# Second gate's products on ScalarE and its sums on GpSimd, and a new order around the first expert selection, in a two-block kernel on one core

## The chip, the cores and the metric

The kernel runs on 1 core of one Trainium2 chip. The metric is the device time of one execution in microseconds (us). An execution with the profiler on gives the rows that are quoted here; its own time stands beside the median of the runs.

## What is computed

256 tokens of width 1024 pass through a first block of two layers and then through a second block (feed-forward, recurrent and attention parts), which the change doesn't touch. In fp32, one layer of the first block is:

```python
mod = c_act @ w_ada[l] + b_ada[l]                    # 1 x 6144
shift1, scale1, gate1, shift2, scale2, gate2 = split(mod, 6)
h = rms_norm(x, norm1_g[l]) * (1 + scale1) + shift1
x = x + gate1 * (concat(attention, convolution, pooling of h @ w_in[l]) @ w_out[l])
h2 = rms_norm(x, norm2_g[l]) * (1 + scale2) + shift2
x = x + gate2 * peer_ffn(h2)
```

In `peer_ffn` each of 8 heads makes a query per token, scores it against two sets of 128 keys, takes the best 16 of each set and the best 16 of their 256 pairs. Each pair is the number of one of 16384 experts. For each token, head and choice, a row of `peer_u` (4 KB) is gathered and multiplied with h2, and a row of `peer_v` is gathered and added up with the gated result.

## The kernel before, in words

Every engine runs its own program; semaphores join them. Line numbers are those of the kernel before.

**Segments of mod.** A segment (1024 columns of `w_ada`) comes in four pieces, q = 0 to 3, of 1 MB each (L495), into the upper halves of the four ring slots. For each half k of a piece, DVE adds piece times a column of `c_act` to a sum held per partition (L2290 in `later_part`, 1024 elements a partition); the first addition starts from `bias_pad`. When all eight are done, `segment_ready` is given, and PE *spreads* the segment: a product with ones adds up the partitions and gives the sum to all of them (`spread`, L1583, 4 rows of the trace). The result is in PSUM, where ScalarE copies it (L952) or DVE takes it with the gain (`scaled_gain`, L2309). A piece's place is given back by `ada_free[q]`, and SP fills it with the next piece in its own fixed order: second gate (GATE2), gain, weights of head 0, next layer's SCALE1, weights of heads 1 to 3, next layer's SHIFT1, weights of heads 4 to 7. SP waits at each for its place.

**From the output rows to the first selection.** PE multiplies the output weights (L1533): first what ends the rows of tile 0 (tokens 0 to 127) and then those of tile 1, with two spreads (L1588) between. DVE, in order: the sums of GATE2 (first piece, `scaled_gain` of SCALE2, three pieces), then per tile: x plus gate times rows (`add_gated`, L2171 and L2173), one sum for the next layer's SCALE1 (`next_first(1)`, L2478), and, when ScalarE has the root mean square (L876, L878), the normalising in two steps (L2114, L2119). ScalarE stands at its copy of SHIFT2 (L952) before it takes tile 0's mean square. PE turns a tile (L1429), makes its queries for head 0 (L1766) and scores them (L1772); between tiles 0 and 1 it spreads GATE2. DVE finds the best keys of tile 0 (L2500 to L2508, per set) and the best pairs (L2513 to L2543), and gives the expert numbers; GpSimd then issues the gathers (L753 for `peer_u`, L759 for `peer_v`), 128 rows or 0.5 MB each.

**After it.** DVE makes six more sums of SCALE1, waits for PE's spread of it (`scaled_gain` from bank 6), makes the eight of SHIFT1, and starts with the dot products (L2577). PE, behind tile 1, waits to spread SCALE1 and then goes through heads 1 to 7 (L1795, `query`; L1808, `key_products`). Part of the gathers has places only when PE is through with a head's weights (`weights_used`). Layer 1 has no next layer in the first block: SCALE1 and SHIFT1 and their spreads fall away there.

**GpSimd** has a convolution and a pooling (L710 to L744) and is then idle up to the first gather.

Of the kernel before, what the change touches and what calls it, by code (L numbers as in the profile page):

```python
# [17 lines left out]
ALU = mybir.AluOpType  # L18
# [9 lines left out]
D = 1024  # L28
KC = D // P
# [46 lines left out]
def program(nc, A, out):  # L76
    with ExitStack() as ctx:
# [3 lines left out]
        def sem(name):  # L81
            return ctx.enter_context(nc.semaphore(name))
# [322 lines left out]
        gelu_ready, rnn_out_ready = sem("gelu_ready"), sem("rnn_out_ready")  # L405
        wf_ready = sem("wf_ready")
        zeroed_for_act = sem("zeroed_for_act")
        f_by_head, f_turned = qk_done, qk_turned
# [60 lines left out]
        def _(sp):  # L469
# [14 lines left out]

            def bias_row(l, segment, pad):
                sp.dma_start(pad[0:1, :], A["b_ada"][l:l + 1, segment * D:(segment + 1) * D]).then_inc(bias_in, 16)

# [27 lines left out]
            for l in range(DEPTH):  # L515
# [37 lines left out]
                for u in range(4):  # L553
                    later_piece(l, SHIFT2, u)
                segment_bias(l, GATE2)
                for q in range(ADA_PAIRS):
                    later_piece(l, GATE2, q)
                w_q = of("peer_wq").rearrange("(k p) n -> p k n", p=P)
# [94 lines left out]
        def _(pool):  # L653
# [53 lines left out]
            for l in range(DEPTH):  # L707
# [35 lines left out]
                pool.sem_inc(pool_steps, -steps.reset())  # L743
                g.tensor_tensor(pooled[:], pooled[:], zc[:, 6:8, :], ALU.subtract).then_inc(pooled_ready, 1)  # L744


# [117 lines left out]
        def _(act):  # L864
# [89 lines left out]
            for l in range(DEPTH):  # L954
# [111 lines left out]
                a.activation(table_use[:], eps[:], ACT.Sqrt).then_inc(act_steps, 1)  # L1066
                act.wait_ge(act_steps, steps.next())
                spread(mod[:, SHIFT2, :], 2)
                norm_x_tile(0)
# [344 lines left out]
        def _(pe):  # L1414
# [167 lines left out]

            def spread(source, bank, give, alone=True):  # L1583

                pe.wait_ge(segment_ready, 1)
                pe.sem_inc(segment_ready, -1)
                for c in range(2):
                    ins = mm(ps[:, bank + c, :], ones[:], source[:, c * N:(c + 1) * N], start=alone, stop=True)  # L1588
                ins.then_inc(give, 1)
# [12 lines left out]
            for l in range(DEPTH):  # L1602
# [176 lines left out]
                first_head(0, w_first)  # L1779
                spread(mod[:, GATE2, :], 2, spread_for_act)  # L1780
                turn_h_tile(1, WORK)
                first_head(1, w_first)
                if l + 1 < DEPTH:
                    spread(mod[:, 0, :], 6, spread_for_dve)
                job = 4
# [26 lines left out]

                query(1)
                for head in range(2, EXPERT_HEADS):
                    query(head)
                    key_products(head - 1)
                    if l + 1 < DEPTH and head == 3:
                        pe.wait_ge(spread_taken, 1)
                        pe.sem_inc(spread_taken, -1)
                        spread(gain_post, 6, spread_for_act)  # L1820
# [270 lines left out]
        def _(dve):  # L2091
# [287 lines left out]
            for l in range(DEPTH):  # L2379
# [73 lines left out]
                more = l + 1 < DEPTH  # L2453
                later_part(0, mod[:, GATE2, :])
                dve.wait_ge(post_in, 16)
# [3 lines left out]
                if l + 1 == DEPTH:  # L2459
                    dve.sem_inc(post_free, 1)  # L2460
                for q in range(1, ADA_PAIRS):
                    later_part(q, mod[:, GATE2, :])
                take_mod()
# [24 lines left out]
                for t in range(TILES):  # L2488
# [6 lines left out]
                    if t == 0:  # L2495
                        take_mod()
                    normalise_tile(t, mod[:, SCALE2, :], mod[:, SHIFT2, :])
                def best_keys(s, scored=half_s):

# [61 lines left out]
                if more:  # L2561
                    next_first(6)
                    dve.wait_ge(pre_in, 16)
# [3 lines left out]
                    dve.sem_inc(u_free, 1)  # L2567
                    next_first(8)
                    assert not first_parts
# [426 lines left out]
```

## Time and profile before

| | |
|---|---|
| median of 3 runs | 2767.92 us (2764.54 to 2772.52) |
| profiled execution | 2766.92 us, span 2765.2 |
| busy over the span | PE 87%, DVE 74%, GpSimd 38%, ScalarE 28% |
| HBM over the span | 293 GB/s |
| layer 0, layer 1 of the first block | about 0 to 840 us, 840 to 1640 us |

The page has a line of slices, each digit the busy share of a fortieth of the span in tenths; it shows in which stretches the DMA engines are full. The view by stretches gives the same for any stretch, with the bytes moved. The timeline gives the instructions of one engine in order of time; in brackets stands how long the engine was idle before, and what ended that. An engine's name with q is its own queue: the wait was for a semaphore at that line.

### The profile page before, as it was taken

The page shows a single profiled execution, that of the slowest core. Times are in us where ns is not written, and L with a number is a line of the kernel's source. Part 1 is how long each engine was busy: PE and PEld are TensorE (multiplying, and loading weights), DVE is VectorE, ACT ScalarE, POOL GpSimd, SP SyncE. Part 2 cuts the span into 40 slices and gives each one's busy share as a digit, 9 for nine tenths or more (in the row PEclk, how much of TensorE's full clock was granted, in tenths as well). Part 3 has the DMA queues.
Part 4 walks back from the last instruction along what each step waited for, and adds up shares of the span by engine and source line. Part 5 has one row for each costly group of instructions (what it writes and reads, how often), then busy time and mean ns, then how long its engine had stood idle before and what let it go on. Part 6 is the DMA issues. An engine that isn't in the chain of part 4 may idle for free. (4 is left out here: it accounts for less than half of the span.)

```text
span 2765.2 us, 31596 instructions
## 1 busy us (share of the span) xinstructions
PE 2401.3 (87%) x9946; PEld 1612.3 (58%) x9946; DVE 2048.1 (74%) x3778; ACT 770.8 (28%) x1088; POOL 1056.0 (38%) x1144
## 2 busy tenths in 40 slices
PE   6979877787778989777778778999999999998998
PEld 5666333333335775333333336888878898887787
DVE  7877788787787876778778777667777656655765
ACT  3422011011012322101100114446543444345443
POOL 1336777777772336777777770002000000000000
PEclk9989998888889999999989889999999999999999
DMA  9789999999999789999999997664466655652564
GB/s 354 253 315 367 409 410 410 409 409 410 410 401 345 253 301 365 409 410 410 409 409 410 410 401 222 195 181 120 141 177 191 191 161 175 190 175 69 158 184 137
DMA packets 424192, 812.71 MB, mean 294 GB/s; under 512 B 26024, under 2 KB 262130, under 8 KB 424094
## 3 DMA queue, kind: packets, MB, share of 16 engines
q0 software_dynamic: 147968, 537.84, 49.2%
q1 hardware_dynamic: 276126, 273.62, 31.3%
q8 instruction: 54, 0.88, 0.1%
q14 instruction: 44, 0.36, 0.0%
HBM read 810.32 MB, written 1.05 MB: 293 GB/s over the span
## 5 line engine op out<-in xcount | busy, mean ns | idle before, releaser
L1833 PE MATMUL ps<-weight_ring,arena 128*128 128x512 f32 x1616 | 810.3, 661 | 254.6 <-PEq L1830 152.2
L1833 PEld LDWEIGHTS ps<-weight_ring,arena 128*128 128x128 f32 x1616 | 339.1, 214 | 720.6 <-issue 720.6
L2577 DVE CUSTOM_DVE_ANT_0 arena<-arena,ps 128x1024 f32<-128x1024 f32 x384 | 455.8, 1218 | 164.5 <-DMA arena<-in_peer_u,expert 145.4
L1466 PE MATMUL ps<-hT_pair,w_hi 128*128 128x512 f32 x1312 | 461.5, 396 | 7.4 <-PEq L1860 7.2
L2137 DVE TENSOR_TENSOR ring_lo<-weight_ring,w_hi 128x3072 fp32r<-128x3072 f32 (+1 forms) x102 | 325.4, 3191 | 172.0 <-DVEq L2136 171.9
L759 POOL DMA_INDIRECT weight_ring<-in_peer_v,expert x390 | 373.0, 956 | 121.2 <-issue 69.6
L753 POOL DMA_INDIRECT arena<-in_peer_u,expert x360 | 341.8, 949 | 134.9 <-issue 54.0
L1465 PE MATMUL ps<-hT_pair,ring_lo 128*128 128x256 f32 x1148 | 320.7, 279 | 0.0
L1466 PEld LDWEIGHTS ps<-hT_pair,w_hi 128*128 128x128 f32 x1312 | 240.8, 188 | 57.1 <-issue 10.1
L921 ACT ACTIVATE w_hi<-weight_ring 128x3072 fp32r<-128x3072 f32 (+1 forms) x102 | 267.7, 2626 | 8.8 <-ACTq L920 8.7
L1130 ACT ACTIVATE acts<-dots 128x8 f32<-128x8 f32 x64 | 13.2, 209 | 865.9 <-ACTq L1129 865.8
L1465 PEld LDWEIGHTS ps<-hT_pair,ring_lo 128*128 128x128 f32 x1148 | 216.6, 189 | 7.1
L2606 DVE TENSOR_SCALAR arena<-ident,acts,gate 128x128 f32<-128x128 f32 x500 | 136.7, 371 | 63.9 <-DVEq L2601 63.9
L860 POOL MEMSET arena<- 128x4096 f32 x1 | 3.5, 3518 | 448.1 <-POOLq L859 448.1
L1457 PE MATMUL ps<-hT_pair,ring_lo 128*128 128x256 f32 (+1 forms) x496 | 139.7, 282 | 0.0
L1203 ACT ACTIVATE arena<-arena 128x256 f32<-128x256 f32 x84 | 35.1, 418 | 307.7 <-ACTq L1202 307.4
L2577 DVE CUSTOM_DVE_ANT_0 weight_ring<-weight_ring,ps 128x1024 f32<-128x1024 f32 x96 | 113.7, 1217 | 5.7 <-DMA weight_ring<-in_peer_u,expert 5.7
L1833 PE MATMUL ps<-hT,arena 128*128 128x512 f32 x256 | 115.2, 593 | 0.5 <-PEq L1830 0.5
L1533 PE MATMUL ps<-w_hi,ff_hi 128*128 128x512 f32 x352 | 109.9, 392 | 0.0
L1533 PE MATMUL ps<-ring_lo,ff_hi 128*128 128x512 f32 x352 | 109.2, 390 | 0.0
L1533 PE MATMUL ps<-w_hi,ff_lo 128*128 128x512 f32 x352 | 109.1, 389 | 0.0
L2727 DVE TENSOR_REDUCE arena<-ps 128x512 f32<-128x1024 f32 x84 | 102.4, 1220 | 4.5 <-DVEq L2726 4.2
(404 smaller groups left out, 3943.6 us busy)
## 6 DMA issues: line engine op xcount, KB each, us to landing
weight_ring<-in_w_ada SPq DMA_DIRECT2D x48, 1024.0 KB, 7.5
weight_ring<-in_ffn_w_gate SPq DMA_DIRECT2D x88, 512.0 KB, 4.0
weight_ring<-in_ffn_w_up SPq DMA_DIRECT2D x88, 512.0 KB, 5.3
weight_ring<-in_ffn_w_down SPq DMA_DIRECT2D x88, 512.0 KB, 5.8
weight_ring<-in_peer_wq SPq DMA_DIRECT2D x16, 1024.0 KB, 9.6
weight_ring<-in_w_in SPq DMA_DIRECT2D x14, 1024.0 KB, 7.7
weight_ring<-in_rg_w_in SPq DMA_DIRECT2D x12, 896.0 KB, 5.2
weight_ring<-in_w_out SPq DMA_DIRECT2D x8, 1024.0 KB, 7.5
```

The source lines that it names most:

```text
L753: g.indirect_dma_start(u_place(l, k), None, A["peer_u"], bass.IndirectOffsetOnAxis(chosen_by[p][:, k:k + 1], 0)).then_inc(u_in[k], 16)
L759: g.indirect_dma_start(v_place(l, k), None, A["peer_v"], bass.IndirectOffsetOnAxis(chosen_by[p][:, k:k + 1], 0)).then_inc(v_in[k], 16)
L921: a.activation(hi[slot][:, 0:width], ring[:, slot, 0:width], ACT.Copy).then_inc(w_hi_ready, 1)
L1457: ins = mm(where, w_low, s_high, start=False, stop=(k == len(pairs) - 1))
L1465: mm(where, w_low, s_high, start=False, stop=False)
L1466: ins = mm(both, w_high, s_pair, start=(k == 0), stop=last)
L1533: ins = mm(ps[:, banks + 2 * t + c, :], source[:, t * P:(t + 1) * P], w[:, c * N:(c + 1) * N], start=start and i == 0, stop=stop and i == ...
L1833: ins = mm(ps[:, 2 * t + c, :], diag[:, k, :], v_place(l, k)[:, c * N:(c + 1) * N], start=False, stop=False, skip_group_check=True)
L2137: v.tensor_tensor(ring_lo[:, slot, 0:width], ring[:, slot, 0:width], hi[slot][:, 0:width].bitcast(F32), ALU.subtract).then_inc(w_split, 1)
L2577: ins = v.tensor_tensor_reduce(out=row, in0=row, in1=h_rows(t), scale=1.0, scalar=0.0, op0=ALU.mult, op1=ALU.add, accum_out=dots[:, g, j:j ...
L2606: v.tensor_scalar(diag[:, k, :], ident[:], acts[:, g, j:j + 1], gate[:, k:k + 1], ALU.mult, ALU.mult).then_inc(diag_ready, 1)
L2727: v.tensor_reduce(gu_sum, banks, AX_X, ALU.add).then_inc(gu_summed, 1)
```

## The change

GATE2's eight products move to ScalarE (each piece times its column, written over the piece), behind its table load and ahead of its copy of SHIFT2. GATE2's eight sums move to GpSimd, behind the pooling, and it gives the pieces' places and the bias row back. The semaphores for it are ones of the second block. PE's spread of GATE2 waits for GpSimd's. DVE, now without GATE2, goes on to `add_gated` of tile 0; three more sums of next layer's SCALE1 follow tile 0's normalising, the rest of them the first selection, and `scaled_gain` comes after half of SHIFT1's sums. PE spreads SCALE1 behind head 1 instead of ahead of it.

```diff
@@ names
+        gate2_in = [gates_ready, root_in, root_ready, gelu_ready]
+        gate2_bias_in, gate2_scaled, gate2_ready = rnn_out_ready, exp_ready, abs_ready
@@ SP
-                segment_bias(l, GATE2)
+                sp.wait_ge(bias_free, 1)
+                sp.sem_inc(bias_free, -1)
+                bias_row(l, GATE2, bias_pad, gate2_bias_in)
                 for q in range(ADA_PAIRS):
-                    later_piece(l, GATE2, q)
+                    sp.wait_ge(ada_free[q], 1)
+                    sp.sem_inc(ada_free[q], -1)
...
+                    sp.dma_start(ada_piece(SLOTS + q), src[:, 2 * q:2 * q + 2, GATE2 * D:(GATE2 + 1) * D]).then_inc(gate2_in[q], 16)
@@ GpSimd, behind the pooling
+                gate2 = mod[:, GATE2, :]
+                pool.wait_ge(gate2_bias_in, 16)
+                pool.sem_inc(gate2_bias_in, -16)
+                for q in range(ADA_PAIRS):
+                    for k in range(2):
+                        pool.wait_ge(gate2_scaled, 1)
+                        pool.sem_inc(gate2_scaled, -1)
+                        g.tensor_tensor(gate2, ada_piece(SLOTS + q)[:, k, :], bias_pad[:] if q == 0 and k == 0 else gate2,
+                                        ALU.add).then_inc(pool_steps, 1)
+                        pool.wait_ge(pool_steps, steps.next())
+                    pool.sem_inc(ada_free[q], 1)
+                    if q == 0:
+                        pool.sem_inc(bias_free, 1)
+                pool.sem_inc(gate2_ready, 1)
+                pool.sem_inc(pool_steps, -steps.reset())
@@ ScalarE
                 act.wait_ge(act_steps, steps.next())
+                for q in range(ADA_PAIRS):
+                    act.wait_ge(gate2_in[q], 16)
+                    act.sem_inc(gate2_in[q], -16)
+                    for k in range(2):
+                        piece = ada_piece(SLOTS + q)[:, k, :]
+                        a.activation(piece, piece, ACT.Copy, scale=c_act[:, 2 * q + k:2 * q + k + 1]).then_inc(gate2_scaled, 1)
                 spread(mod[:, SHIFT2, :], 2)
                 norm_x_tile(0)
@@ PE
-                spread(mod[:, GATE2, :], 2, spread_for_act)
+                spread(mod[:, GATE2, :], 2, spread_for_act, ready=gate2_ready)
                 turn_h_tile(1, WORK)
                 first_head(1, w_first)
-                if l + 1 < DEPTH:
-                    spread(mod[:, 0, :], 6, spread_for_dve)
...
                 query(1)
+                if l + 1 < DEPTH:
+                    spread(mod[:, 0, :], 6, spread_for_dve)
                 for head in range(2, EXPERT_HEADS):
@@ DVE
-                later_part(0, mod[:, GATE2, :])
                 dve.wait_ge(post_in, 16)
...
-                for q in range(1, ADA_PAIRS):
-                    later_part(q, mod[:, GATE2, :])
                 take_mod()
...
                     normalise_tile(t, mod[:, SCALE2, :], mod[:, SHIFT2, :])
+                    if t == 0:
+                        next_first(3)
...
                 if more:
-                    next_first(6)
+                    next_first(3)
+                    next_first(4)
                     dve.wait_ge(pre_in, 16)
                     dve.sem_inc(pre_in, -16)
                     scaled_gain(gain_pre[:], 6, gain_pre[:])
                     dve.sem_inc(spread_taken, 1)
                     dve.sem_inc(u_free, 1)
-                    next_first(8)
+                    next_first(4)
```

## Rows read from the trace of the kernel before

**Rows 1.** Stretches; columns: stretch, length, busy of each engine (count), PEclk, DMA share, GB/s.

```profile
158.00:170.00 12.00, 7.78 (x50) 6.08 (x50) 9.99 (x28) 3.79 (x9) 1.25 (x1) 0.99 0.00 0
...
230.00:240.00 10.00, 9.98 (x58) 8.94 (x57) 10.00 (x25) 2.59 (x6) 5.46 (x6) 1.00 0.71 231
240.00:250.00 10.00, 9.22 (x25) 4.26 (x24) 3.04 (x8) 1.83 (x3) 7.56 (x9) 1.00 0.95 339
250.00:800.00 550.00, 429.82 (x884) 182.03 (x883) 432.81 (x1111) 50.47 (x96) 412.22 (x432) 0.88 1.03 410
```

**Rows 2.** Timeline, DVE, layer 0: start us, us, instruction [idle before <-releaser].

```profile
126.70 1.28 DVE L2290 SCALAR_TENSOR_TENSOR arena<-weight_ring,c_act,bias_pad 128x1024 f32<-128x1024 f32 x1 [0.47 <-DVEq L2287]
...
137.00 2.60 DVE L2290 SCALAR_TENSOR_TENSOR arena<-weight_ring,c_act,arena 128x1024 f32<-128x1024 f32 x2 [0.26 <-DVEq L2287]
...
152.78 1.29 DVE L2119 TENSOR_TENSOR h_ext<-h_ext,arena 128x512 f32<-128x512 f32 x2
...
159.35 0.29 DVE L2500 MAX8 best<-arena 128x8 f32<-128x128 f32 x1 [2.65 <-DVEq L2555]
...
161.19 0.42 DVE L2513 TENSOR_TENSOR arena<-best 128x256 f32<-128x256 f32 x1
...
167.25 0.23 DVE L2543 TENSOR_SCALAR first_expert<-expert_f,expert_base 128x16 uint32<-128x16 f32 x1
...
180.29 1.23 DVE L2309 SCALAR_TENSOR_TENSOR gain_pre<-ps,gain_pre 128x1024 f32<-128x1024 f32 x1 [4.57 <-DVEq L2308]
...
193.78 1.22 DVE L2577 CUSTOM_DVE_ANT_0 arena<-arena,ps 128x1024 f32<-128x1024 f32 x1 [0.50 <-DVEq L2626]
```

**Rows 3.** Timeline, PE, layer 0.

```profile
128.69 7.03 PE L1533 MATMUL ps<-weight_ring,hT 128*128 128x512 f32 x16
...
137.28 7.03 PE L1533 MATMUL ps<-weight_ring,hT 128*128 128x512 f32 x16
146.66 1.23 PE L1429 MATMUL ps<-ident,h_ext 128*128 128x128 f32 x8 [2.36 <-PEq L1427]
148.92 3.76 PE L1766 MATMUL ps<-hT,weight_ring 128*128 128x128 f32 x16 [1.02 <-PEq L1764]
...
158.62 1.88 PE L1588 MATMUL ps<-arena,ones 128*128 128x512 f32 x4
...
162.92 2.02 PE L1766 MATMUL ps<-hT,weight_ring 128*128 128x128 f32 x16 [1.55 <-PEq L1764]
...
179.57 15.19 PE L1795 MATMUL ps<-hT,weight_ring 128*128 128x256 f32 x64
...
223.38 7.15 PE L1795 MATMUL ps<-hT,weight_ring 128*128 128x256 f32 x32 [1.24 <-PEq L1793]
```

**Rows 4.** Timeline, ACT, layer 0.

```profile
137.56 1.02 ACT L952 ACTIVATE arena<-ps 128x1024 f32<-128x1024 f32 x1 [15.05 <-ACTq L951]
142.69 1.06 ACT L876 ACTIVATE h_ext<-x 128x1024 f32<-128x1024 f32 x1 [4.11 <-ACTq L882]
```

**Rows 5.** Landing of the ada piece issued at 129.9 and head weights issued at 190.6.

```profile
DMA to landing us min/median/max: 9.4/9.4/9.4
...
DMA to landing us min/median/max: 32.5/32.5/32.5
```

**Rows 6.** Timeline, layer 0: POOL, and a DVE instruction beside the second row.

```profile
90.58 0.72 POOL L718 TENSOR_TENSOR arena<-arena 128x255 f32<-128x255 f32 x1
...
97.92 1.26 POOL L724 TENSOR_TENSOR hT<-arena 128x512 f32<-128x512 f32 x1
...
104.07 1.14 POOL L737 TENSOR_TENSOR arena<-arena 128x570 f32<-128x570 f32 x1
...
111.29 2.02 POOL L744 TENSOR_TENSOR arena<-arena 128x512 f32<-128x512 f32 x1 [0.18 <-POOLq L743]
...
97.99 1.22 DVE L2219 TENSOR_TENSOR sink_d<-sink,row_max 128x4 f32<-128x4 f32 x1
```

**Rows 7.** Timeline, PE, layer 1: turning tile 0.

```profile
978.89 1.23 PE L1429 MATMUL ps<-ident,h_ext 128*128 128x128 f32 x8 [1.67 <-PEq L1427]
```

More of the change, by code:

```diff
@@ L483, in load_gain, with bias_row @@
                 sp.dma_start(gain[:], A[name][l:l + 1].to_broadcast([P, D])).then_inc(given, 16)
-            def bias_row(l, segment, pad):
-                sp.dma_start(pad[0:1, :], A["b_ada"][l:l + 1, segment * D:(segment + 1) * D]).then_inc(bias_in, 16)
+            def bias_row(l, segment, pad, given=bias_in):
+                sp.dma_start(pad[0:1, :], A["b_ada"][l:l + 1, segment * D:(segment + 1) * D]).then_inc(given, 16)
             def segment_bias(l, segment):
@@ L554, in _ @@
                     later_piece(l, SHIFT2, u)
-                segment_bias(l, GATE2)
+                sp.wait_ge(bias_free, 1)
+                sp.sem_inc(bias_free, -1)
+                bias_row(l, GATE2, bias_pad, gate2_bias_in)
                 for q in range(ADA_PAIRS):
-                    later_piece(l, GATE2, q)
+                    sp.wait_ge(ada_free[q], 1)
+                    sp.sem_inc(ada_free[q], -1)
+                    src = A["w_ada"][l].rearrange("(p k) n -> p k n", k=KC)
+                    sp.dma_start(ada_piece(SLOTS + q), src[:, 2 * q:2 * q + 2, GATE2 * D:(GATE2 + 1) * D]).then_inc(gate2_in[q], 16)
                 w_q = of("peer_wq").rearrange("(k p) n -> p k n", p=P)
@@ L1581, in attend, with spread @@
                 pe.sem_inc(attn_done, -2)
-            def spread(source, bank, give, alone=True):
-                pe.wait_ge(segment_ready, 1)
-                pe.sem_inc(segment_ready, -1)
+            def spread(source, bank, give, alone=True, ready=segment_ready):
+                pe.wait_ge(ready, 1)
+                pe.sem_inc(ready, -1)
                 for c in range(2):
```

## The prediction

> **What bounds the kernel now.** I read the page's slices first, for where the DMA engines are full, and then took the stretches apart by time. From 250 to 800 us, the expert stage of layer 0, the gathers move 410 GB/s at a DMA share of 1.03, while PE, DVE and POOL are each below 80% busy [rows 1]. In that stretch nothing that an engine saves can show. What can show is when the stage gets going: the DMA engines do nothing at all between 158 and 170 us, and move only 231 GB/s from 230 to 240 and 339 from 240 to 250 [rows 1]. Layer 1 has the same stage. So I price the change by what it takes out of these holes, in DMA time: a piece of 1.05 MB at 410 GB/s is 2.5 us.
>
> Next I followed DVE, in order of time, to the first selection. It works through the second gate from 126.70 to 139.6 us [rows 2], although PE had the first half of its products of 128.69 to 135.7, and with it the output rows of tile 0, near 132.3 [rows 3]. Tile 1 is normalised at 154.1, the keys' second half begins at 159.35, the pairs at 161.19, and the first expert numbers come at 167.25. Then there are six next-layer sums, 4.57 us of waiting for PE's spread of the scale, eight more sums, and the first dot product at 193.78 [rows 2]. PE turns tile 0 at 146.66 after 2.36 us of idleness, needs 3.76 us for 16 products of its head where tile 1's take 2.02, spreads the second gate at 158.62, and starts head 1 only at 179.57 [rows 3].
>
> **The change, part by part.** *Second gate off DVE.* Eight sums of 1.28 to 1.30 us and the small waits between, together about 11 us [rows 2]. ScalarE is idle for 15.05 us up to 137.56, and its square of the same width takes 1.06 us [rows 4]: eight products are 8.5 us. DVE had the last piece by 137.00 [rows 2]; had it landed only then, ScalarE's last two products would end at 139.1 and hold back its SHIFT2 copy by 1.6 us. The piece is issued at about 126.4, so it was probably there by 133: I take nothing, bound 1.6.
>
> *The sums on GpSimd.* None of them is 1024 wide before. A 255-wide addition takes 0.72 us and a 570-wide one 1.14 [rows 6], so 1.33 ns an element more, and 1024 come to 1.75 us. A 512-wide product takes 1.26 [rows 6], twice that is 2.5. I take 2.1, keep 1.75 and 2.5 as bounds, and 4.05 (twice the crowded 2.02 [rows 6]) as the far one. The Trainium skill (GPSIMD Engine Reference, Elementwise — side-by-side cycle accounting) gives 4497 ns for 2048 elements. By it one sum would take, as an estimate, 2.25 us; that lies between my bounds.
>
> These sums hold DVE up too. At 97.99 DVE's subtraction of 4 elements takes 1.22 us and ends as GpSimd's product of 97.92 ends [rows 6]. GpSimd's own 512-wide subtraction takes 2.02 where the product takes 1.26 [rows 6]. By these rows the two wait out each other's instructions. The Trainium skill (SBUF — State Buffer, Who interferes with whom) has the rule: a VectorE instruction with two inputs in SBUF and a GpSimd instruction that reads SBUF exclude each other, each for the other's whole length. By this rule the change gives back part of what it takes off DVE, and the trace agrees, with the 1.22 us.
>
> So I walked from 124 us on with strict alternation. DVE's last SHIFT2 sum waits about 2 us. GpSimd is through with the four pieces at 130.4, 134.8, 140.3 and 145.7 (at 1.75 us a sum: 129.7, 133.3, 138.1, 141.7). DVE takes tile 0 up at 132.5 and has x by 136; ScalarE has its mean square at 137.56 + 1.02 + 1.5 = 140.1. But the next-layer sum ahead of the normalising wants a piece that landed 9.4 us after its issue at 129.9 [rows 5], at 139.3, and it and the two normalising steps each meet a GpSimd sum. h of tile 0 is ready at 145.1 to 147.6, before at 146.6. PE is through with the output rows at 144.3 [rows 3]. **Tile 0 gains 1.4 us at best and loses 1 at worst**; without the lock it would gain 2.4. Tile 1 now stands behind three more sums, 3.9 us, and is normalised at 156.6 to 159.1 instead of 154.1. With 1.84 us for each half of the keys [rows 2] the pairs begin at 160.3 to 162.8, before at 161.19. The first gather thus comes 0.9 us earlier to 1.6 later; with no lock and quick products of PE, 3.3 earlier. **I take 0.**
>
> *SP's queue.* The next-layer pieces now wait for GpSimd: the fourth goes out up to 6 us later, and heads 1 to 3 behind it. They are wanted after 165, so that costs nothing. But the first two SCALE1 pieces are consumed by about 148, ahead of the keys, so the second SHIFT1 piece is fetched in the empty stretch of 158 to 170 us and no longer among the gathers: **2.5 us**.
>
> *After the first selection.* DVE has three sums left for the scale, not six, and does four of SHIFT1 while PE runs head 1; the 4.57 us of waiting go. From 167 to 169 us, eleven sums, the scaled gain and a wait or two for the last pieces bring the first dot product to 184 to 188, 6 to 9 us ahead of 193.78. PE starts head 1 at about 167.5 and spreads the scale behind it at 175. Its later heads wait for weights: the one at 223.38 [rows 3] was issued at 190.6 and took 32.5 us to land [rows 5]. Their places come free 6 to 9 us earlier. So the openings on which GpSimd's gathers wait come about 7 us earlier, and the DMA backlog ends 2.5 earlier. From 230 to 240 us there lack 10 x (1 - 231/410) = 4.4 us of DMA time [rows 1], and the difference, 7 - 2.5 = 4.5, covers it: **4.4 us**. Bounds: 0, and 6.1 with the lack of 240 to 250.
>
> *Layer 1* has no next-layer sums. PE turns tile 0 at 978.89 after 1.67 us of idleness [rows 7]. GpSimd's sums begin near 958 and end at 973.4 to 977.5, so PE turns 0.6 to 1.7 us earlier: **1.0 us**, bounds 0.3 and 3.3 (the upper one with quick products of PE).
>
> **Sum:** 0 + 2.5 + 4.4 + 1.0 = 7.9 us. The profiled execution took 2766.92 us (its span is 2765.2, 1.7 lie around it): 2759.0. The median of the runs shown, 2767.92, is 1.0 above that execution and would give 2760.0. I forecast 2759.5.
>
> **Rivals.** (1) *The lock is weak and GpSimd quick.* Tile 0 goes to PE at 144.3 without a pause, and its products take 2.0 us instead of 3.76 [rows 3]. The first gather gains 3.3, layer 0 is held by openings that come 9 us earlier, layer 1 gives 3: 2767.4 - 12 = 2755.5. For it: DVE's instructions that read PSUM aren't held up. Against: the 1.22 us. (2) *A full DMA hides it.* The openings would come earlier, but the heads' weights, queued among the gathers, land no sooner. What is left is 2.5 + 1.0, less a first gather that comes 1 us late: 2765. For it: the 32.5 us. This is also how the change would not do what it says. (3) *Slower: the second gate becomes the bound.* PE spreads it ahead of turning tile 1, at 158.62 [rows 3], and in layer 1 about 10 us behind the turning of 978.89 [rows 7]. From 125 and 958 us on that leaves room for eight sums of 4.2 and of 3.8 us. Beyond that every query of PE stands behind the wait, and the next-layer pieces starve DVE. At 5 us a sum the third piece is free at 155 and refilled at 162, so the first gather comes 9 us later, less 2.5, and layer 1's queries 8 later: 2767.4 + 14 = 2781. For it: the crowded 2.02 us; against: every other row.
>
> **How the numbers follow.** Forecast 0.45, rival 1 0.22, rival 2 0.20, rival 3 0.13. 0.3% is 8.3 us, about what a measurement can tell from no change. The forecast's own range, 2756 to 2763, lies across that bound; 0.20 of its 0.45 count as faster, 0.25 as the same. Faster: 0.20 + 0.22 = 0.42. Same: 0.25 + 0.20 = 0.45. Slower: 0.13. The range takes in rivals 1 and 2 and the 3 to 4 us by which the runs scatter, and leaves out rival 3: 2753 to 2770.
>
> **What would show it.** GpSimd's 1024-wide additions at 1.75 to 2.5 us, some longer by DVE's 1.28; DVE's sums between 124 and 146 us stretched up to 3.4; PE turning tile 0 between 144.3 and 148; expert numbers within 2 us of 167.25; the first dot product at 184 to 188; over 350 GB/s from 230 to 240. The prediction is wrong if the first gather comes over 3 us earlier (the lock), if the head of 223.38 still starts after 221 (the weights), or if PE waits for the second gate ahead of tile 1.

## The result, and the profile after

The changed kernel takes 2774.86 us (median of 20 runs, 2770.04 to 2780.17), the kernel before 2768.52 (20 runs beside them): a ratio of 1.0022, 95% interval 1.0015 to 1.0029, some 6 us slower. That lies inside the 0.3% that were taken for no change, but on the slower side and outside the forecast range of 2753 to 2770. The profiled execution is the fastest of the 20 (2770.04 us, span 2768.3). It shows 3.1 us of the difference; where the rest lies in the other executions isn't shown.

Line numbers are now those of the changed kernel: L2200 and L2202 are `add_gated`, L2143 and L2148 the normalising, L2504 a next-layer sum, L760 GpSimd's sums of the second gate, L1458, L1795 and L1801 PE's turning, first head and scoring.

The stretches, with the columns of [rows 1]:

```profile
145.00:158.00 13.00, 6.70 (x27) 4.82 (x25) 11.70 (x8) 2.76 (x6) 3.53 (x2) 0.74 0.80 275
158.00:170.00 12.00, 8.67 (x48) 7.03 (x48) 10.05 (x34) 3.16 (x8) 0.00 (x0) 0.86 0.82 297
...
230.00:240.00 10.00, 9.27 (x50) 8.20 (x49) 10.00 (x25) 1.95 (x5) 4.69 (x5) 1.00 0.81 276
240.00:250.00 10.00, 9.20 (x30) 4.73 (x30) 3.41 (x8) 2.47 (x5) 7.31 (x8) 1.00 0.89 289
250.00:800.00 550.00, 431.34 (x887) 182.04 (x885) 432.38 (x1109) 49.13 (x94) 411.40 (x432) 0.88 1.03 409
```

The empty stretch from 158 to 170 us is filled, at 297 GB/s instead of 0. The hole from 230 to 250 is as large as it was: 276 and 289 GB/s, before 231 and 339. The stage itself still moves 409 GB/s.

DVE's timeline in layer 0, where [rows 2] stood:

```profile
134.37 1.23 DVE L2200 TENSOR_TENSOR h_ext<-ps,arena 128x1024 f32<-128x1024 f32 x1 [2.20 <-DVEq L2516]
135.62 1.56 DVE L2202 TENSOR_TENSOR x<-x,h_ext 128x1024 f32<-128x1024 f32 x1
...
143.81 5.47 DVE L2148 TENSOR_TENSOR h_ext<-h_ext,arena 128x512 f32<-128x512 f32 x2
149.21 1.27 DVE L2504 SCALAR_TENSOR_TENSOR arena<-weight_ring,c_act,arena 128x1024 f32<-128x1024 f32 x1
...
155.05 1.23 DVE L2202 TENSOR_TENSOR x<-x,h_ext 128x1024 f32<-128x1024 f32 x1
...
159.53 1.29 DVE L2148 TENSOR_TENSOR h_ext<-h_ext,arena 128x512 f32<-128x512 f32 x2
...
163.76 0.29 DVE L2528 MAX8 best<-arena 128x8 f32<-128x128 f32 x1 [1.23 <-DVEq L2583]
...
171.67 0.23 DVE L2571 TENSOR_SCALAR first_expert<-expert_f,expert_base 128x16 uint32<-128x16 f32 x1
...
182.62 1.23 DVE L2338 SCALAR_TENSOR_TENSOR gain_pre<-ps,gain_pre 128x1024 f32<-128x1024 f32 x1 [0.63 <-DVEq L2337]
...
190.19 1.22 DVE L2606 CUSTOM_DVE_ANT_0 arena<-arena,ps 128x1024 f32<-128x1024 f32 x1 [0.51 <-DVEq L2655]
```

GpSimd beside it, its first, sixth and last sum, and the first gather:

```profile
125.91 2.36 POOL L760 TENSOR_TENSOR arena<-weight_ring,bias_pad 128x1024 f32<-128x1024 f32 x1 [12.98 <-POOLq L759]
...
139.60 3.09 POOL L760 TENSOR_TENSOR arena<-weight_ring,arena 128x1024 f32<-128x1024 f32 x1 [0.20 <-POOLq L759]
...
146.19 2.54 POOL L760 TENSOR_TENSOR arena<-weight_ring,arena 128x1024 f32<-128x1024 f32 x1 [0.20 <-POOLq L759]
172.97 1.24 POOL L776 DMA_INDIRECT arena<-in_peer_u,first_expert  x1 [24.24 <-POOLq L775]
```

PE, where [rows 3] stood:

```profile
146.68 0.63 PE L1458 MATMUL ps<-ident,h_ext 128*128 128x128 f32 x4 [0.45 <-PEq L1456]
149.43 1.09 PE L1458 MATMUL ps<-ident,h_ext 128*128 128x128 f32 x4 [2.12 <-PEq L1456]
...
151.54 3.76 PE L1795 MATMUL ps<-hT,weight_ring 128*128 128x128 f32 x16 [1.02 <-PEq L1793]
158.41 0.46 PE L1801 MATMUL ps<-keysT,arena 128*128 128x128 f32 x2 [3.11 <-PEq L1800]
...
173.60 7.14 PE L1822 MATMUL ps<-hT,weight_ring 128*128 128x256 f32 x32
180.59 1.88 PE L1617 MATMUL ps<-arena,ones 128*128 128x512 f32 x4
...
223.62 7.14 PE L1822 MATMUL ps<-hT,weight_ring 128*128 128x256 f32 x32 [1.41 <-PEq L1820]
```

And ScalarE: its first products, tile 1's mean square, and the copy for which PE's scoring waits:

```profile
124.58 4.27 ACT L1096 ACTIVATE weight_ring<-weight_ring,c_act 128x1024 f32<-128x1024 f32 x4
...
156.40 1.06 ACT L899 ACTIVATE h_ext<-x 128x1024 f32<-128x1024 f32 x1 [5.16 <-ACTq L905]
...
157.78 0.26 ACT L1111 ACTIVATE arena<-ps 128x128 f32<-128x128 f32 x1
```

Read together: DVE takes tile 0 up early, at 134.37, as planned. But the two halves of its last normalising step, 1.29 us together in [rows 2], take 5.47: each of them waits out one of GpSimd's sums. PE has turned the first half of tile 0 at 147.3 and stands 2.12 us for the second. Then DVE makes its three extra sums, so x of tile 1 is written at 155.05; ScalarE waits 5.16 us for it, and the copy of tile 0's first queries stands in its queue behind that, so PE's scoring stands 3.11 us. Tile 1 is normalised at 160.8 (before, 154.1), the second half of the keys is another 1.23 us of waiting, the expert numbers come at 171.67 (167.25), the first gather starts at 172.97, 4.4 us later than before (168.55). After it the plan holds: the scale's spread costs 0.63 us of waiting instead of 4.57, and the first dot product starts 3.6 us earlier, at 190.19. Yet the head of 223.38 starts at 223.62.

Layer 0 ends, by its last `x` of tile 1, at 864.92 against 863.04, 1.9 us later. That would fit the 4.4 us of the gather less the 2.5 of the piece that now fills the empty stretch, but it is one execution of each kernel and doesn't show it. Layer 1 shows the first half of the pattern once more, and its first gather is another 1.5 us late (1001.73 against 998.38, less the 1.9):

```profile
976.31 5.47 DVE L2148 TENSOR_TENSOR h_ext<-h_ext,arena 128x512 f32<-128x512 f32 x2
```

### The profile page after: what moved, and what is told of

Its sections match the earlier page's. It is cut to its first block and busy times, and to the rows that moved or that the text cites. A ratio compares the mean times of both kernels' runs of the same rounds, so it can differ in the third digit from the quotient of the medians.

```text
span 2768.3 us, 31630 instructions
## 1 busy us (share of the span) xinstructions
PE 2403.7 (87%) x9946; PEld 1611.2 (58%) x9946; DVE 2041.0 (74%) x3762; ACT 787.9 (28%) x1104; POOL 1099.7 (40%) x1160
## 5 line engine op out<-in xcount | busy, mean ns | idle before, releaser
L1822 PE MATMUL ps<-hT,weight_ring 128*128 128x256 f32 x448 | 102.1, 388 | 5.9 <-PEq L1820 5.2
```

The costliest lines, as they stand in the source:

```text
L1822: ins = mm(ps[:, job % 4, 0:SEQ], w[:, k, c * P:(c + 1) * P], hT[:, k, :], start=(k == 0), stop=(k == KC - 1))
```

## The experiments

They ran on three chips on which the DMA engines move 354 to 361 GB/s in the expert stage, where they moved 409 and 410 for the two kernels above, and all kernels take some 200 us more. Every ratio is against the kernel before on the same chip; it is the ratio on record, and not quite the quotient of the two medians. Up to 200 us the kernel before has nearly the same timeline there (first gather 167.82 against 168.55, first dot product 193.04 against 193.78; in between up to 2 us apart), so landmarks can be compared to a microsecond or two; the ratio tells the time. Each landmark comes from one execution. Two kernels without any edit show that. In the fences below the rows of one kernel's timeline, of several engines, stand in order of time.

**The kernel before, unchanged.**

> The kernel before, unchanged, for a profile on the chip of this series. Landmarks as in its first profile: first gather at 168.5 us, head 1 at 179.6, first dot product at 193.8, each within 2 us; ratio 1.000.

2974.36 us, ratio 1.0006 (0.9987 to 1.0025). First gather at 167.82. (The median of the same kernel's 35 runs beside it is 2977.51: this is how far equal kernels lie apart.)

**The changed kernel, unchanged.**

> The changed kernel as it is, beside the same before kernel as the others of this series, so that its ratio and its landmarks can be read against theirs on one chip. Theory (GpSimd's sums hold both halves of the normalising step, the three sums hold up tile 1, and either alone costs the whole gain): ratio 1.001 to 1.003; the first gather at about 173.6, 5 to 6 us behind the 167.82 of the before kernel. Rival (the slower second gate only shows on the first chip, as chance): ratio within 0.001 of 1.

2980.13 us, ratio 1.0006 (0.9987 to 1.0024); first gather at 172.90, 5.1 us later than the one above, and in layer 1 at 1101.48 against 1096.05, 5.4 us later. The expected 1.001 to 1.003 is met by the interval only, and the ratio itself is the rival's; the delay is there again, its price is smaller or hidden in the scatter of this chip.

**No three sums.** The changed kernel, with all of the next layer's sums behind the selection again:

```diff
                     normalise_tile(t, mod[:, SCALE2, :], mod[:, SHIFT2, :])
-                    if t == 0:
-                        next_first(3)
...
-                    next_first(3)
+                    next_first(6)
                     next_first(4)
```

> The changed kernel, but the three next-layer sums between tile 0 and tile 1 stand behind the first selection again (six there instead of three). Theory A: in the changed kernel these three sums push x of tile 1 to 156.3 us, and ScalarE, whose mean square of tile 1 stands ahead of its first copy of tile 0's queries, makes PE wait 3.11 us at 158.41. Then here PE has no such wait, the first gather is issued 2 to 4 us earlier than the changed kernel's 172.97, and the ratio to the kernel before falls from 1.0022 to about 1.0010. Theory B: only GpSimd's hold on DVE counts (5.47 us for the two halves of the second normalising step instead of 1.29). Then the first gather stays within 1 us of 172.97 and the ratio at 1.002 or above, since DVE reaches its first dot product later.

2967.8 us, ratio 1.0018 (1.0002 to 1.0035). 

```profile
142.63 1.60 DVE L2504 SCALAR_TENSOR_TENSOR arena<-weight_ring,c_act,bias_pad 128x1024 f32<-128x1024 f32 x1 [6.89 <-DVEq L2502]
...
147.54 3.31 DVE L2148 TENSOR_TENSOR h_ext<-h_ext,arena 128x512 f32<-128x512 f32 x2
...
150.40 1.84 PE L1458 MATMUL ps<-ident,h_ext 128*128 128x128 f32 x8 [5.27 <-PEq L1456]
...
158.79 0.29 DVE L2526 MAX8 best<-arena 128x8 f32<-128x128 f32 x1 [0.98 <-DVEq L2581]
...
161.76 0.29 DVE L2526 MAX8 best<-arena 128x8 f32<-128x128 f32 x1 [1.16 <-DVEq L2581]
...
170.96 1.23 POOL L776 DMA_INDIRECT arena<-in_peer_u,first_expert  x1 [21.25 <-POOLq L775]
```

The wait at the scoring is gone (0.73 us), x of tile 1 is written at 152.03, and still the first gather gains only 2 us, and the ratio stays at 1.0018 where theory A had 1.0010. Here DVE stands 6.89 us for the next-layer piece ahead of tile 0's normalising: GpSimd's second sum, itself 3.11 us long, ends at 131.8 and frees the place, the piece is issued at 132.7 and takes 9.7 us to land. What follows is again stretched by the sums. PE turns tile 0 from 150.40, where in the changed kernel it had the first half at 146.68 and the second at 149.43, and DVE waits 0.98 and 1.16 us for the two halves of its keys. The run "The split alone", below, is the same program up to the selection; there the piece is issued at 130.9, lands 7.8 us later, the wait is 2.25 us and the first gather comes at 168.94. So 2 us of this gather are the scatter of single executions.

**One sum only.** The changed kernel with seven of GpSimd's eight sums left out:

```diff
                     for k in range(2):
...
-                        g.tensor_tensor(gate2, ..., bias_pad[:] if q == 0 and k == 0 else gate2, ALU.add)
-                        pool.wait_ge(pool_steps, steps.next())
+                        if q == 0 and k == 0:
+                            g.tensor_tensor(gate2, ..., bias_pad[:], ALU.add)
+                            pool.wait_ge(pool_steps, steps.next())
```

> The changed kernel with seven of GpSimd's eight sums of the second gate left out (the second gate is then wrong); ScalarE's products, every semaphore and DVE's order stay. It takes away what holds DVE up and what makes the places come free late. Theory B: tile 0 is turned at 144.3 to 145, x of tile 1 comes near 150, the first gather at 165 to 167, and the ratio falls to 0.9955 to 0.9975. Theory A (the three sums and ScalarE's order are the larger part): tile 0 is early all the same, but x of tile 1 and the first gather come no more than 2 us ahead of the changed kernel's, ratio above 1.000.

2959.0 us, ratio 0.9989 (0.9975 to 1.0002).

```profile
145.22 1.29 DVE L2148 TENSOR_TENSOR h_ext<-h_ext,arena 128x512 f32<-128x512 f32 x2
...
155.60 0.77 PE L1801 MATMUL ps<-keysT,arena 128*128 128x128 f32 x2 [3.72 <-PEq L1800]
...
161.85 0.29 DVE L2528 MAX8 best<-arena 128x8 f32<-128x128 f32 x1 [2.08 <-DVEq L2583]
...
171.06 1.24 POOL L776 DMA_INDIRECT arena<-in_peer_u,first_expert  x1 [41.11 <-POOLq L775]
```

With the sums gone the halves take 1.29 us and `add_gated` and the rest have their old lengths: it is GpSimd's sums, not ScalarE's products or the placement, that stretch them. But the three sums are still between the tiles, x of tile 1 comes at 152.28, PE's scoring waits 3.72 us behind ScalarE's mean square, DVE waits 2.08 for the keys that come of it, and the first gather again gains only 2 us. That is the other theory's forecast; the gather at 165 to 167 and the ratio of 0.9955 to 0.9975 were misses. In part it is this execution: DVE takes the scale's gain at 132.6, 1.7 us later than in the changed kernel, ahead of anything that the two suspects touch.

**Neither.** Both edits together:

> The changed kernel with both suspects gone: no next-layer sums between the tiles, and seven of GpSimd's eight sums left out (the second gate is then wrong). With the changed kernel (both there), the one without the three sums and the one with a single sum this makes a square of four. If the two suspects explain the first gather, it comes at 164.5 to 167 here, against 170.96 and 171.06 with one of them and 172.97 with both. If something else delays it (ScalarE's products, later landings), it stays above 168.

2970.16 us, ratio 0.9975 (0.9957 to 0.9993).

```profile
148.44 2.02 PE L1795 MATMUL ps<-hT,weight_ring 128*128 128x128 f32 x16 [1.07 <-PEq L1793]
...
152.49 1.29 DVE L2148 TENSOR_TENSOR h_ext<-h_ext,arena 128x512 f32<-128x512 f32 x2
...
164.89 1.25 POOL L776 DMA_INDIRECT arena<-in_peer_u,first_expert  x1 [35.43 <-POOLq L775]
```

This closes the square of the two suspects. The first number of a place is when DVE has tile 1 normalised and turns to the keys, the second how long it then waits for the keys, the third the first gather, all in us:

| | GpSimd's eight sums | one sum |
|---|---|---|
| three sums between the tiles | 160.8, 1.1, 172.90 | 158.0, 2.1, 171.06 |
| none between | 157.8, 2.1, 170.96 | 153.7, 0.2, **164.89** |

Taking either suspect away brings 2 us here, taking both 8. (With the 168.94 of the split alone in the lower left place it brings 4, and without the 1.7 us of late start the one sum brings 3.5: each alone is worth 2 to 4 us.) DVE's own part is nearly a plain sum: the lock makes tile 1 late by 4.1, the three sums by 4.3, both by 7.1. The rest is in the waits. With either suspect left, tile 0's keys are late as well (with the lock because PE gets tile 0 late, with the three sums because ScalarE's mean square of tile 1 stands ahead of tile 0's copy), and of the 3 us that DVE gets back it spends 1 waiting for them. Only with both gone are the keys there when DVE is. The square has two things in one of its suspects: without its sums GpSimd also gives the pieces' places back earlier. The stretched halves are the lock, since their own lengths show it; how much of the gather is the later places and not the lock isn't shown.

**The copy ahead of the mean square.** The changed kernel, with ScalarE's mean square of tile 1 behind tile 0's first query and key copies:

```diff
                 evacuate_hT_tile(0, hT, WORK)
-                norm_x_tile(1)
...
                             fan(act, key_s_ready)
+                        if t == 0 and c == 0:
+                            norm_x_tile(1)
```

> The changed kernel with one exchange on ScalarE: tile 1's mean square stands behind the copies of tile 0's first query and key half, not ahead of them. Theory A (ScalarE's order turns the late tile 1 into a late tile 0): PE's wait of 3.1 to 3.7 us between the first query product and its scoring falls to about 0.7, the second key half comes some 3 us earlier, and the first gather goes from 172.97 to 170 or 171; DVE, whose tile 1 ends at 160.8, keeps it from going lower. Ratio 1.0005 to 1.0018. Theory B (only GpSimd's hold counts): PE's wait goes, but the first gather stays above 172.

2978.62 us, ratio 1.0006 (0.9990 to 1.0022). The wait at the scoring goes, from 3.11 to 0.73 us, and with it DVE's wait for the keys' second half, from 1.12 (the changed kernel above) to 0.17:

```profile
156.75 0.77 PE L1802 MATMUL ps<-keysT,arena 128*128 128x128 f32 x2 [0.73 <-PEq L1801]
...
164.43 0.29 DVE L2529 MAX8 best<-arena 128x8 f32<-128x128 f32 x1 [0.17 <-DVEq L2584]
```

From the start of the keys to the first gather it is 11.2 us (162.46 to 173.64) instead of 12.1 (160.77 to 172.90), so ScalarE's order costs 1 us. The expected gather at 170 to 171 was a miss all the same, and by its number theory B's. Tile 1 came 1.7 us later, which took the gain back: this whole execution is 1.2 us behind from the start (DVE takes the scale's gain at 132.13 against 130.98), and the mean square, now behind the copies, makes DVE wait 1.07 us for it instead of 0.54. Counted from that gain, the exchange brings the gather 0.4 us. What bounds the gather is DVE's tile 1.

**The new order alone.** The kernel before, with PE's spread of the scale behind head 1 and DVE's sums 10, gain, 4 as in the changed kernel:

```diff
                 first_head(1, w_first)
-                if l + 1 < DEPTH:
-                    spread(mod[:, 0, :], 6, spread_for_dve)
...
                 query(1)
+                if l + 1 < DEPTH:
+                    spread(mod[:, 0, :], 6, spread_for_dve)
...
                     next_first(6)
+                    next_first(4)
...
-                    next_first(8)
+                    next_first(4)
```

> The kernel before with one part of the change: PE spreads the next scale behind head 1, and DVE takes the scaled gain after half of SHIFT1's sums. The second gate stays on DVE. If the later part of my sum was right, the 4.57 us of waiting go, the first dot product comes at about 189 instead of 193.78, head 1 starts at about 169.2 instead of 179.57, the first gather stays at 168.5, and the whole gains 3 to 5 us: ratio 0.9980 to 0.9990. If a full DMA hides it (the heads' weights land no sooner), the ratio is 0.9995 to 1.0005.

2962.38 us, ratio 1.0005 (0.9988 to 1.0023). The scale's wait is 0.38 us, the first dot product starts at 191.27 and head 1 at 168.97, 10 us earlier than the 178.84 of the kernel before on such a chip. But the later heads stand longer for their weights, and the head of 223.38 (which is its time in both executions of the kernel before) starts at 224.59. The interval still leaves room for a gain of 3 us; the landmarks show none:

```profile
200.39 9.57 PE L1793 MATMUL ps<-hT,weight_ring 128*128 128x256 f32 x32 [5.16 <-PEq L1791]
213.18 7.14 PE L1793 MATMUL ps<-hT,weight_ring 128*128 128x256 f32 x32 [2.33 <-PEq L1791]
224.59 8.83 PE L1793 MATMUL ps<-hT,weight_ring 128*128 128x256 f32 x32 [3.37 <-PEq L1791]
```

**The split alone.** The kernel before, with the second gate on ScalarE and GpSimd and nothing else of the change (the order of PE and DVE behind the first selection as before, no sums between the tiles). Against the changed kernel:

```diff
                 first_head(1, w_first)
+                if l + 1 < DEPTH:
+                    spread(mod[:, 0, :], 6, spread_for_dve)
...
                     normalise_tile(t, mod[:, SCALE2, :], mod[:, SHIFT2, :])
-                    if t == 0:
-                        next_first(3)
...
-                    next_first(3)
-                    next_first(4)
+                    next_first(6)
...
-                    next_first(4)
+                    next_first(8)
```

> The kernel before with the other part alone: second gate's products on ScalarE, its sums on GpSimd; no sums between the tiles, the scale's spread and the fourteen remaining sums as in the kernel before. Theory B (GpSimd's hold on DVE eats the gain): h of tile 0 at 148 to 150 us instead of 147, first gather 0 to 2 us later than 168.55, first dot product 0 to 2 later than 193.78, ratio 1.0005 to 1.0020. If the hold were harmless and only the three sums harmed, tile 0 would be turned at 144 to 146 and the ratio would be 0.9990.

2965.81 us, ratio 1.0019 (1.0005 to 1.0034). The halves take 5.47 us again (at 143.52), the first gather starts at 168.94, the first dot product at 193.86. So even alone, with DVE free of eight sums, the split brings the gather no earlier than the kernel before has it (168.55, 167.82 and 168.49 in three executions), and the time is longer. A first gather that is hardly late doesn't explain a time 0.2% longer; layer 1, at the end of this section, does better.

**On DVE, in its gaps.** The kernel before, with the second gate's sums left on DVE but moved into its waits: the first two pieces behind tile 0's `add_gated`, one behind tile 1's, the last behind tile 1's normalising.

```diff
-                    next_first(1)
+                    later_part(2 * t, mod[:, GATE2, :])
                     if t == 0:
+                        later_part(1, mod[:, GATE2, :])
                         take_mod()
                     normalise_tile(t, mod[:, SCALE2, :], mod[:, SHIFT2, :])
+                    if t == 1:
+                        later_part(3, mod[:, GATE2, :])
```

> The kernel before with another way to take tile 0 up at once: the second gate's sums stay on DVE but stand in the gaps (pieces 0 and 1 while ScalarE makes tile 0's mean square, piece 2 in tile 1's, piece 3 behind tile 1's normalising); all sixteen next-layer sums come after the selection. No work on GpSimd, no hold, nothing between tile 0 and tile 1 but the rest of a gap. If hold and order are the whole reason for the loss, tile 0 is turned at 144.3 to 145, the first gather issued at 164 to 166.5 instead of 168.5, and the ratio is 0.9980 to 0.9992. If what counts is how early the pieces' places come free (they do later here), the gather is early and the ratio all the same 1.000 or above.

2982.2 us, ratio 1.0007 (0.9987 to 1.0028). Tile 0 goes to PE without a wait and its head takes 2.02 us, but the second gate is now late for PE, and DVE has the same work ahead of the selection and comes to the keys only at 157.84: gather at 169.03 (164 to 166.5 was expected, a miss), first dot product at 199.49.

```profile
157.79 3.75 PE L1588 MATMUL ps<-arena,ones 128*128 128x512 f32 x4 [2.87 <-PEq L1586]
```

**Summed by PE.** The complete form of the run with neither suspect. ScalarE writes its products to a place of their own, as operands of PE, and frees the pieces itself; PE adds all of them as it spreads them. GpSimd has no part in it.

```diff
@@ ScalarE
-                        a.activation(piece, piece, ACT.Copy, scale=c_act[...]).then_inc(gate2_scaled, 1)
+                        ins = a.activation(prod[:, 2 * q + k, :], ada_piece(SLOTS + q)[:, k, :], ACT.Copy, scale=c_act[...])
+                    ins.then_inc(ada_free[q], 1)
@@ PE
-                spread(mod[:, GATE2, :], 2, spread_for_act, ready=gate2_ready)
+                for k in (KC, *range(KC)):
+                    for c in range(2):
+                        ins = mm(ps[:, 2 + c, :], prod_one[:], prod[:, k, c * N:(c + 1) * N], start=(k == KC), stop=(k == KC - 1))
```

> The changed kernel without its three early next-layer sums, and with the second gate summed by PE: ScalarE multiplies the pieces into a place of its own (it frees each pair of a piece at once), and PE adds the eight products and the bias up in PSUM as it spreads them, 18 matmuls of 512 columns instead of 2. GpSimd does nothing of it, so no sum holds DVE up, and nothing is left out. It is the complete form of the run with neither suspect. Theory (what counts is when DVE is through with tile 1): the normalising halves take 1.29 us again, the pairs begin near 157.5, the first gather comes at 164 to 166, the first dot product at 186 to 190, and the time is 0.9960 to 0.9985 of before. Tile 1's head ends 1 to 5 us later than in that run (158 to 164 us is PE's), which costs nothing. Rival (full DMA decides from the first gather on, and an earlier gather only waits longer at its openings): the gather comes at 165 and the ratio is 0.999 to 1.001. Other rival (PE's 18 matmuls take over 8 us and hold back head 1 and the scale's spread): head 1 after 172, the first dot product after 193, ratio 1.000 to 1.002.

2968.35 us against 2974.1: a ratio of **0.9977 (0.9961 to 0.9994)**, the one complete kernel that is faster than both.

```profile
147.01 2.02 PE L1790 MATMUL ps<-hT,weight_ring 128*128 128x128 f32 x16 [1.10 <-PEq L1788]
...
151.03 1.29 DVE L2148 TENSOR_TENSOR h_ext<-h_ext,arena 128x512 f32<-128x512 f32 x2
...
153.06 4.37 PE L1808 MATMUL ps<-prod,prod_one 128*128 128x512 f32 x18
...
163.53 1.24 POOL L763 DMA_INDIRECT arena<-in_peer_u,first_expert  x1 [50.69 <-POOLq L762]
```

The 18 products take 4.37 us, where the 4 rows of the spread took 1.88 [rows 3]; PE has room for them. The first gather comes 4.3 us earlier than in the kernel before on such a chip (167.82), in layer 1 6.2 us earlier (1089.87 against 1096.05). The first theory of that expectation holds in the normalising halves, the first dot product (186.51) and the ratio; the gather came 0.5 us ahead of its range. This kernel differs from the changed one in three things together: no sums on GpSimd, no three sums between the tiles, and earlier places for the pieces.

**Layer 1, and the time.** The three sums and the new order don't exist in layer 1; there the kernels differ only in where and when the second gate's sums are made (and "copy first" in ScalarE's order). The table has, for each execution, the first gather of layer 0, how long after the end of layer 0 the first gather of layer 1 starts, and the ratio:

| kernel | first gather, layer 0 | from the end of layer 0 to the first gather of layer 1 | ratio |
|---|---|---|---|
| before (sums on DVE) | 167.82 | 136.6 | 1.0006 |
| new order alone (sums on DVE) | 168.49 | 137.4 | 1.0005 |
| on DVE, in its gaps | 169.03 | 135.9 | 1.0007 |
| changed (eight sums on GpSimd) | 172.90 | 140.1 | 1.0006 |
| no three sums (eight) | 170.96 | 140.1 | 1.0018 |
| split alone (eight) | 168.94 | 140.1 | 1.0019 |
| copy first (eight) | 173.64 | 142.1 | 1.0006 |
| one sum only | 171.06 | 131.9 | 0.9989 |
| neither | 164.89 | 134.3 | 0.9975 |
| summed by PE | 163.53 | 132.0 | 0.9977 |

The first gather of layer 0 doesn't order the times: "no three sums" and "one sum only" have it 0.1 us apart, on one chip, and their medians are 8.8 us apart (2967.8 and 2959.0). In layer 1 the kernels with eight sums on GpSimd start 3 to 6 us later than those with the sums on DVE, and those without the sums 2 to 5 us earlier. So GpSimd's sums cost in both layers, the three sums in one.

## Why the prediction was wrong

The forecast was a gain of 7.9 us; the profiled execution is 3.1 us longer, 11 us away. Two steps carry 8.8 of these: the first gather, taken as 0 and 4.4 us late, and the openings, taken as 4.4 us of gain and worth nothing. Layer 1, taken as 1.0 us of gain and 1.5 late, carries the rest.

**The first step that failed is "I take 0"** for the first gather. It came 4.4 us later; the bounds of the sum reached to 1.6. Three terms of it were short:

- *GpSimd's sum.* Taken as 2.1 us, it takes 2.36 where nothing is in its way and 3.0 to 3.1 beside DVE. Eight of them ended at 148.7 and not at 145.7. The length was inside the bounds of 1.75 to 2.5, and the 2.25 us estimated from the Trainium skill's figure (GPSIMD Engine Reference, Elementwise — side-by-side cycle accounting) is nearer to the trace than what I took. The longer sums aren't the whole of it: at 2.36 us each, the eighth would by my estimate still have run until 146.5, past the 143.81 at which tile 0's halves began.
- *What the lock does to a step in halves.* I let the normalising steps "each meet a GpSimd sum". The second of them is two instructions, and each of the two waited for one: 5.47 us for 1.29 of work. h of tile 0 was ready at 149.3; I had 145.1 to 147.6. With one sum in place of eight it is 1.29 again. The rule that the Trainium skill gives (SBUF — State Buffer, Who interferes with whom) is thus borne out; what I had wrong was how often it bites.
- *Tile 1.* I had it normalised at 156.6 to 159.1; it was 160.8, since the three sums begin only when the stretched halves end. I also took the pairs as bound by DVE alone and did not look at ScalarE's queue. There tile 1's mean square stands ahead of tile 0's query copy, a wait of 3.11 us for PE, of which about 1 us reaches the gather, as the run with the copy first shows. The far end of the bounds, 1.6 us late, would be 170.2; with that 1 us and the 1.7 by which tile 1 passed 159.1 it is 172.9, where the gather was.

**The 4.4 us of the openings failed as well, and by rival 2.** Both signs named for it came: the head of 223.38 starts after 221, at 223.62, and 230 to 240 us moves 276 GB/s and not over 350. The rival's mechanism was right: the heads' weights were issued 3 to 6 us earlier and landed no sooner. The load for which the head of 223.38 waits was issued at 190.6 and took 32.5 us [rows 5]; now it is issued at 187.0, and the view of landings has

```profile
weight_ring<-in_peer_wq SPq DMA_DIRECT2D x1, 1024.0 KB, 36.4
```

that is, both land at 223. The next one took 37.8 us from 194.3, and before 30.3 from 197.6: it lands 4 us later. The run with the new order alone is the test: dot products and head 1 earlier, by 2 and 10 us, a ratio of 1.0005. I gave this rival 0.20, although the row of 32.5 us was in my hands: 1 MB at 410 GB/s is 2.5 us, so the load spends the other 30 beside and behind other traffic, and the earlier issue didn't shorten that.

**What held.** The empty stretch was filled: 0 GB/s became 297. That this is worth the 2.5 us of the piece isn't shown. Layer 0 ends 1.9 us late where the gather was 4.4 late, but single executions don't carry such a difference: "no three sums" and "one sum only" have their gathers 0.1 us apart and end layer 0 at 966.27 and 953.95. DVE's 4.57 us of waiting went. The first dot product came 3.6 us earlier, not 6 to 9 (184 to 188 forecast, 190.19 measured), and all of the miss is the later selection. ScalarE's products were done at 134.2 and held nothing up: the SHIFT2 copy, at 139.49, waited for PE's spread. PE did not wait for the second gate ahead of tile 1, so rival 3 did not occur.

**Layer 1** was to gain 1.0 us and lost 1.5 by the first gather, and 2.3 by the end of its stage (1680.53 against 1676.39, less the 1.9 of layer 0); on the chips of the experiments it lost 3.5 by the first gather. GpSimd's sums, forecast to end at 973.4 to 977.5, end at 981.2, and the halves take 5.47 us there too.

With measured terms the sum is +4.4 for the gather, 0 for the openings and +1.5 to +2.3 for layer 1, 5.9 to 6.7 us in all. The medians differ by 6.3. The profiled execution is 3.1 us longer, which leaves room for the 2.5 of the piece; the medians leave none. Which of the two is right stays open.

**Rival 1** (quick products of PE, a gather 3.3 us early) describes well what is to be had: in the run with the sums on PE the 16 products of tile 0 take 2.02 us and not 3.76, and the gather gains 4.3. It needs the sums away from GpSimd and the three sums away from between the tiles: with one sum only, tile 0's products take 2.02 us too, and the gather still comes at 171.06.

## What to carry to other kernels

Moving work to an idle engine isn't free when that engine shares something with the busy one: count how many of the busy engine's instructions lie beside the moved ones, each half of a split step for itself, and let each wait for up to a whole instruction of the other. Test suspects also together, not only one at a time: here either one left in place kept 4 to 6 of the 8 us. Look at every layer that has the change, not only at the one with the clearest landmark, and don't read 2 us out of single executions. The earlier issue of loads that stood in full DMA gained nothing here.

## What the runs showed of the hardware

- DVE's SBUF-to-SBUF additions and GpSimd's additions take strict turns: two 512-wide halves (0.65 us each alone) took 5.47 us beside two 1024-wide GpSimd sums, and GpSimd's sums beside DVE's SBUF-to-SBUF instructions grew from 2.36 to between 2.5 and 3.1 (to 3.4 in the run without the three sums). DVE's sums that read PSUM were not stretched (L2200, 1.23 us at 134.37, beside a running sum).
- The same 16 products of PE take 2.02 us where PE comes to them out of its output rows without a pause longer than 1.1 us (147.01 and 148.44 above), and 3.76 where it had stood idle: 5.27 us in the run without the three sums, 2.12 in the changed kernel, 2.36 in the one before. The granted clock during the 3.76 us is 0.50 of full speed (the lower level, 1.2 GHz), during the 2.02 us it is 1.00 (2.4 GHz). After 1.59 us of idleness, in the kernel before on another chip, they take 3.37 us at a mean of 0.57. Part of what an earlier tile 0 brings is this.
- PE's 128x512 products take 4.37 us for 18 in the rounded fp32 form (0.24 us each) with both operands written by ScalarE; the full fp32 spread takes 1.88 us for 2.
- From 176 to 196 us of the changed kernel the gathers moved 5.39 MB and SP's loads 2.62 MB of the 8.02: the loads of weights got about a third of a full DMA there.
- The expert stage's DMA moved 410 GB/s in the first measurement and 354 to 361 on the three chips of the experiments, in the same kernel and with nearly the same time up to there. What makes the difference isn't shown.
